# Hybrid decoder layer in fp32: product 5 of the convolution groups divided a second time

## What is computed

```python
h = rmsnorm(x, norm_g[layer])
proj = h @ w_in[layer]
b_a, c_a, x_a, z_a, q, k, v, z_b, g_a, g_b = jnp.split(proj, split_points, axis=-1)
# short_conv_branch
u = c_gate * xv
u = causal depthwise conv, 3 taps, + conv_b
y = b_gate * u * jax.nn.silu(z)
```

## Time and profile before

| | us |
|---|---|
| median of 3 runs | 1365.33 |
| lowest and highest | 1364.96, 1366.29 |
| profiled execution | 1364.82 |
| its span, first to last instruction | 1363.0 |
| TensorE busy | 1351.7 (99%) |
| VectorE busy | 1037.9 (76%) |
| ScalarE busy | 607.5 (45%) |
| GpSimd busy | 350.8 (26%) |

### The profile page before, as it was taken

One profiled execution on the slowest core, in us unless ns is written; L12 is line 12 of the kernel. 1 busy time (PEld: TensorE's weight loads), 2 busy tenths in 40 slices (PEclk: granted clock), 3 DMA queues, 4 the chain that ended last, 5 costly groups with the idle time before them and its releaser, 6 DMA issues.

```text
span 1363.0 us, 17225 instructions
## 1 busy us (share of the span) xinstructions
PE 1351.7 (99%) x6642; PEld 1143.1 (84%) x6642; DVE 1037.9 (76%) x1089; ACT 607.5 (45%) x823; POOL 350.8 (26%) x341
## 2 busy tenths in 40 slices
PE   9999999999999999999999999999999999999997
PEld 8788888888888888888888888888888888888886
DVE  7898466677777777677877777748776998788887
ACT  7843233433333333333433333438778443434445
POOL 0100122343444444223222233325544001100002
PEclk9999999999999999999999999999999999999999
DMA  9736545334443343466656556767767699935443
GB/s 343 214 126 213 152 107 169 89 103 109 109 109 84 102 108 94 131 177 177 178 157 174 149 156 183 216 209 252 269 217 263 151 331 306 237 152 201 165 83 124
DMA packets 112978, 234.80 MB, mean 172 GB/s; under 512 B 7680, under 2 KB 50816, under 8 KB 108032
## 3 DMA queue, kind: packets, MB, share of 16 engines
q1 hardware_dynamic: 104112, 194.87, 42.0%
q0 software_dynamic: 8640, 38.80, 16.0%
q10 hardware_dynamic: 144, 0.02, 0.0%
HBM read 169.70 MB, written 55.57 MB: 165 GB/s over the span
## 4 chain that ended last, share of the span: by engine, by line
PE 92%; ACT 2%; DVE 2%; issue 2%; DMA 1%; POOL 1%; SPq 1%; POOLq 0%; ACTq 0%; DVEq 0%
PE psum L2591 15%; PE psum L2593 15%; PE psum L2594 15%; PE psum L2732 7%; PE psum L2734 7%; PE psum L2733 7%; PE psum L2517 3%; PE psum L2519 3%; PE psum L2518 3%; PE psum L2506 3%; PE psum L2509 3%; PE psum L2508 3%; PE psum L2636 2%; PE psum L2638 2%; PE psum L2637 2%
## 5 line engine op out<-in xcount | busy, mean ns | idle before, releaser
L1126 ACT ACTIVATE slots<-work 128x1024 fp32r<-128x1024 f32 (+1 forms) x166 | 169.5, 1027 | 418.5 <-PE psum L2594 284.8
L2591 PE MATMUL psum<-hc,slots 128*128 128x512 f32 x912 | 354.9, 389 | 0.0
L2593 PE MATMUL psum<-hc,slots 128*128 128x512 f32 x912 | 354.9, 389 | 0.0
L2594 PE MATMUL psum<-hc,slots 128*128 128x512 f32 x912 | 354.8, 389 | 0.0
L2594 PEld LDWEIGHTS psum<-hc,slots 128*128 128x128 f32 x912 | 171.2, 188 | 35.7
L2591 PEld LDWEIGHTS psum<-hc,slots 128*128 128x128 f32 x912 | 171.3, 188 | 34.9
L2593 PEld LDWEIGHTS psum<-hc,slots 128*128 128x128 f32 x912 | 171.2, 188 | 34.8
L1412 ACT ACTIVATE last_slot<-arena 128x1024 fp32r<-128x1024 f32 x112 | 118.6, 1062 | 163.1 <-PE psum L2734 157.3
L2732 PE MATMUL psum<-last_slot 128*128 128x512 f32 (+1 forms) x452 | 175.3, 388 | 0.0
L2734 PE MATMUL psum<-last_slot 128*128 128x512 f32 (+1 forms) x452 | 175.0, 387 | 0.0
L2733 PE MATMUL psum<-last_slot 128*128 128x512 f32 (+1 forms) x452 | 175.0, 387 | 0.0
(11 more groups left out here) (225 smaller groups left out, 2424.1 us busy)
## 6 DMA issues: line engine op xcount, KB each, us to landing
work<-w_channel SPq DMA_DIRECT2D x80, 512.0 KB, 4.3
work<-w_channel POOLq DMA_DIRECT2D x40, 512.0 KB, 5.5
arena<-w_last SPq DMA_DIRECT2D x19, 1024.0 KB, 7.4
qk<-qk_scratch SPq DMA_DIRECT2D x32, 512.0 KB, 3.5
arena<-w_last POOLq DMA_DIRECT2D x9, 1024.0 KB, 11.0
v_raw<-value_scratch SPq DMA_DIRECT2D x32, 256.0 KB, 3.8
arena<-gate_scratch SPq DMA_DIRECT2D x16, 512.0 KB, 6.6
value_c<-w_value SPq DMA_DIRECT2D x10, 512.0 KB, 4.7
```

What stands on the lines that cost most here:

```text
L1126: nc.scalar.activation(slots[:, u % SLOTS, 0, 0:columns_of(u)], src, ACT.Copy, scale=-1.0 if negated(u) else 1.0).then_inc(w_hi, 1)
L2591: nc.tensor.matmul(bank, slot[:, 0, w], x_high, start=product in STARTS and j == 0, stop=False, skip_group_check=True)
L2593: nc.tensor.matmul(bank, slot[:, 0, w], x_low, start=False, stop=False, skip_group_check=True)
L2594: last = nc.tensor.matmul(bank, slot[:, 1, w], x_high, start=False, stop=j == 3, skip_group_check=True)
```

## The change

Product 5 is divided in the convolution groups (`FIFTHS = CONVS`). It gets a second unit, `FIFTH_HALF`, right behind its first; its T1, T2 and T4 lie in `hx`, where product 4's lie. So both sets are made in groups 0 and 1 and stored in DRAM (`hx_d`), and `hx` is loaded twice in every convolution group, for product 5 when product 4 of the group before has ended, for product 4 when product 5 has ended. T3 takes the place of a quarter of `hc`, saved and loaded back.

The sum S1 is no longer made by GpSimd from b and d, but by a transfer that adds quadrant 2 onto e, which is now loaded with quadrant 3 by itself; d is loaded separately, later. In convolution groups this transfer is issued ahead of GpSimd's sums for products 4 and 3, whose order is exchanged. GpSimd's sums for product 5 stand between its two products with the gate. VectorE's order changes: product 5's first slot right behind product 2's, the first tap waits for product 5's sums, product 5's second slot stands between the taps, the slots of products 7 and 3 follow the first subtraction of product 5, and product 4's first slot stands within its second subtractions. On ScalarE c11 moves behind product 3's first slot, and one SiLU of two columns is added at the start of group 2.

```diff
@@ -49,9 +49,10 @@
-LAST_HALF, THIRD_HALF = 7, 8
-UNIT_TABLE = [(g, p) for g in range(GROUPS) for p in (0, 1, 2, 3, 4, 5, 6, LAST_HALF, THIRD_HALF)
-              if (p != THIRD_HALF or g in THIRDS) and (p != LAST_HALF or g in TWICE)]
+FIFTHS = CONVS
+LAST_HALF, THIRD_HALF, FIFTH_HALF = 7, 8, 9
+UNIT_TABLE = [(g, p) for g in range(GROUPS) for p in (0, 1, 2, 3, FIFTH_HALF, 4, 5, 6, LAST_HALF, THIRD_HALF)
+              if (p != THIRD_HALF or g in THIRDS) and (p != LAST_HALF or g in TWICE) and (p != FIFTH_HALF or g in FIFTHS)]
...
 def halved_product(g, product):
 
-    return product == 4 and g in TWICE or product == 3 and g in THIRDS
+    return product == 4 and g in TWICE or product == 3 and g in THIRDS or product == 5 and g in FIFTHS
...
     g, n = place_of(u)
-    return 3 * QUARTER if n in (5, 6) and halved_product(g, product_at(n)) else 2 * HALF
+    return 3 * QUARTER if n in (3, 5, 6) and halved_product(g, product_at(n)) else 2 * HALF
...
@@ -189,10 +212,10 @@
 ROLES = [dict(a=0, b=1, c=2, d=3, e=4)]
 for _ in range(GROUPS - 1):
     r = ROLES[-1]
-    ROLES.append(dict(a=r["c"], b=r["b"], c=r["a"], d=r["e"], e=r["d"]))
+    ROLES.append(dict(a=r["c"], b=r["b"], c=r["a"], d=r["d"], e=r["e"]))
...
+    hx_d = nc.dram_tensor("hx_scratch", (2, P, 3, 2, 2, QUARTER), F32, kind="Internal").ap()
+    kept_d = nc.dram_tensor("kept_scratch", (4, P, 2, 2, QUARTER), F32, kind="Internal").ap()
...
     def second_bank(g, product):
 
-        return set_at(g + 1, 1 if g in THIRDS and product == 4 else 6)
+        return set_at(g + 1, 1 if product == 5 or g in THIRDS and product == 4 else 6)
...
+        def load_hx(product):
+            n = int(product == 5)
+            sp.dma_start(hx[:, 2].bitcast(F32), hx_d[n, :, 2]).then_inc(t4_in, 16)
+            sp.dma_start(hx[:, 0:2].bitcast(F32), hx_d[n, :, 0:2]).then_inc(t1_t2_in, 16)
+
         for g in range(GROUPS):
+            if g == 1:
+                sp.wait_ge(h_ready, made(3) + 4)
+                for part, a in enumerate((t5_high, t5_low)):
+                    sp.dma_start(hx_d[1, :, :, part], a[:, 0:3]).then_inc(fifth_kept, 16)
+                    sp.dma_start(kept_d[3, :, part], a[:, 3]).then_inc(fifth_kept, 16)
+                sp.wait_ge(fifth_kept, 112)
+                sp.wait_ge(h_ready, made(3) + 4 + 3)
+                sp.dma_start(hx_d[0], hx[:, :].bitcast(F32)).then_inc(fifth_kept, 16)
+            if g == FIFTHS.start:
+                sp.wait_ge(unit_done, unit_at(g - 1, 5) + 1)
+                sp.wait_ge(fifth_kept, 128)
+                for part in range(2):
+                    sp.dma_start(x_quarter(5, 1, part).bitcast(F32), kept_d[3, :, part]).then_inc(fifth_kept, 16)
+            if g in FIFTHS:
+                sp.wait_ge(unit_done, ended_at(g - 1) + 1)
+                load_hx(5)
+            if g == FIFTHS.stop:
+                sp.wait_ge(unit_done, fifth_ended_at(g - 1) + 1)
+                for part in range(2):
+                    sp.dma_start(x_quarter(5, 1, part).bitcast(F32), kept_d[2, :, part]).then_inc(fifth_kept, 16)
             if g == THIRDS.start:
                 stores[kind_of(g - 1)](g - 1)
             if g + 1 < GROUPS:
                 sp.wait_ge(w_ready, unit_at(g, 2) + 1)
-                sp.wait_ge(summed, summed_until(g) + 2)
+                sp.wait_ge(summed, s2_made(g))
                 load_work(g + 1, "a", 0)
...
             if g + 1 < GROUPS:
-                sp.wait_ge(w_ready, unit_at(g, 5) + 1)
-                load_work(g + 1, "d", 3)
+                sp.wait_ge(w_ready, fifth_ended_at(g) + 1)
+                load_work(g + 1, "e", 3)
                 sp.wait_ge(w_ready, unit_at(g, 7) + 1)
                 load_work(g + 1, "b", 2)
                 if g in THIRDS and g > THIRDS.start:
                     stores[kind_of(g - 1)](g - 1)
+                if g in FIFTHS:
+                    sp.wait_ge(unit_done, fifth_ended_at(g) + 1)
+                    load_hx(4)
+                if g in THIRDS:
+                    sp.wait_ge(w_ready, ended_at(g) + 1)
+                    load_work(g + 1, "d", 3)
                 sp.wait_ge(w_ready, third_ended_at(g) + 1)
                 load_work(g + 1, "c", 1)
             if g and g not in THIRDS:
                 stores[kind_of(g - 1)](g - 1)
+            if g + 1 < GROUPS and g not in THIRDS:
+                sp.wait_ge(w_ready, ended_at(g) + 1)
+                load_work(g + 1, "d", 3)
...
         def s1(g):
-            a, b, c, d, e = buffers(g)
+
+            if g:
+                work_loaded(g, "e")
+                pool.dma_start(work[ROLES[g]["e"]][:, :], w_channel[g, 2], accum_op=ALU.add).then_inc(s1_in, 16)
+            else:
+                a, b, c, d, e = buffers(g)
+                work_loaded(g, "b")
+                work_loaded(g, "d")
+                pool.wait_ge(w_ready, unit_of(1, 3, 1) + 1)
+                nc.gpsimd.tensor_tensor(e, b, d, ALU.add).then_inc(summed, 1)
+
+        def s3(g):
+
             work_loaded(g, "b")
-            work_loaded(g, "d")
-            pool.wait_ge(w_ready, ended_at(g - 1) + 1 if g else unit_of(1, 3, 1) + 1)
-            nc.gpsimd.tensor_tensor(e, b, d, ALU.add).then_inc(summed, 1)
-
-        def s3(g):
-
-            pool.wait_ge(summed, summed_until(g) + 1)
+            if g == 0:
+                pool.wait_ge(summed, summed_until(g) + 1)
             pool.dma_start(work[ROLES[g]["b"]][:, :], w_channel[g, 0], accum_op=ALU.add).then_inc(s3_in, 16)
 
         def s2(g):
             a, b, c, d, e = buffers(g)
+            if g:
+                pool.wait_ge(s1_in, 16 * g)
             pool.wait_ge(w_ready, unit_at(g, 1) + 1)
             nc.gpsimd.tensor_tensor(a, e, a, ALU.add).then_inc(summed, 1)
...
@@ -993,13 +1065,20 @@
             conv = g > 0 and kind_of(g - 1) == "conv"
             if conv:
                 conv_gate(g - 1, 1)
+            if g in FIFTHS:
+                second_sums(g, 5)
+            if conv:
                 conv_gate(g - 1, 2)
+            if g in FIFTHS:
+                s1(g + 1)
             if g in THIRDS:
+                second_sums(g, 4)
                 second_sums(g, 3)
-            if g in TWICE:
+            elif g in TWICE:
                 second_sums(g, 4)
             if g + 1 < GROUPS:
-                s1(g + 1)
+                if g not in FIFTHS:
+                    s1(g + 1)
                 s3(g + 1)
                 s2(g + 1)
...
-                    if product in (5, 6):
-                        act.wait_ge(summed, summed_until(g) + (5, 6).index(product) + 1)
+                    if product == 6:
+                        act.wait_ge(summed, s2_made(g))
+                    elif product == 5:
+                        act.wait_ge(s1_in if g else summed, 16 * g if g else summed_until(g) + 1)
...
+        def fifth_high():
+
+            act.wait_ge(t_made, 12 + 8)
+            for n in range(4):
+                nc.scalar.activation(t5_high[:, n].bitcast(F32R), t5_low[:, n], ACT.Copy).then_inc(h_hi, 1)
...
@@ -1558,8 +1648,11 @@
                 first(g)
             if p == 1 and g - 1 in CONVS:
                 first_tap(g - 1)
-            if p == 3:
+            if p == (FIFTH_HALF if g in FIFTHS and kind == "conv" else 3):
                 c11(g)
+            if g == CONVS.start and p == 1:
+                act.wait_ge(conv_step, 1)
+                nc.scalar.activation(u_pad[:, 0:CONV - 1], u_pad[:, 0:CONV - 1], ACT.Silu)
...
-        def second_rest(g, product):
-
-            dve.wait_ge(unit_done, (ended_at(g) if product == 4 else third_ended_at(g)) + 1)
+        def second_rest(g, product, parts=range(3)):
+
+            dve.wait_ge(unit_done, halved_ended_at(g, product) + 1)
             z = second_bank(g, product)
             to = flat((tp_v if product == 4 else tp_first)[g % 2][:, :, :]).rearrange("p (n c) -> p n c", n=4)
-            for n, (quarters, bank, c) in enumerate(((slice(1, 4), z, 0), (slice(1, 4, 2), z + 1, 0),
-                                                     (slice(2, 4), z + 1, QUARTER))):
+            for n in parts:
+                quarters, bank, c = ((slice(1, 4), z, 0), (slice(1, 4, 2), z + 1, 0), (slice(2, 4), z + 1, QUARTER))[n]
                 if n:
                     dve.wait_ge(value_sum, second_added(g, product, 1 + n))
...
@@ -2060,6 +2167,18 @@
                 g, n = place_of(u - 1)
                 if n in (5, 6) and halved_product(g, product_at(n)):
                     second_first(g, product_at(n))
+                    if n == 6 and g in FIFTHS and g not in THIRDS:
+                        low(u + 1)
+                elif n == 3 and halved_product(g, 5):
+                    second_first(g, 5)
+                elif n == FIFTH_HALF:
+                    second_rest(g, 5, range(1))
+                    if g in THIRDS:
+                        low(u + 2)
+                    second_rest(g, 5, range(1, 3))
+                    add(g, 5)
+                    if g not in THIRDS:
+                        low(u + 2)
```

(74 more changed lines are left out.)

63 lines of the change are left out of this document (41 added, 22 removed).

## The result

| | before | after |
|---|---|---|
| median, us | 1365.33 | 1368.54 |
| lowest and highest of 13 runs, us | 1364.89, 1367.01 | 1367.30, 1369.38 |
| profiled execution, us | 1364.82 | 1368.66 |
| its span, us | 1363.0 | 1366.8 |

What follows compares the result with a forecast made beforehand. TensorE, busy 1351.7 of 1363.0 us, was taken to bound the kernel. 1364.82 - 4.0 (matmuls) + 0.3 (one-off costs, late hx loads) = 1361.1 us profiled, 1361.6 as median; range 1360.6 to 1368.0.

Steps and rivals of the forecast that it cites:

- Removed matmuls: Product 5 divided on TensorE: 0.50 us less in each of eight groups, 4.0 us in all, at least 3.4.
- The work added on VectorE, ScalarE and GpSimd: Rearranged slots, sums and copies in each convolution group: costs nothing if the margins hold; the group ends at 36.68 us.
- the thinnest: VectorE's sum for product 5, done 4.9 us after product 7's start (Y), wanted at Y+5.44: 0.5 us to spare.
- Rival B: Product 5's chain on VectorE or ScalarE runs late for product 3 or 7; 0.5 us per group gives 1365.6; chance 0.16.
- The load of hx for product 4: Second hx load per convolution group: lands at Y+9.5 (Y: product 7's start), 0.2 us ahead of use; bounds Y+7.5, Y+11.7.
- Rival A: hx comes late, so TensorE stands before product 4's second half, eight times; chance 0.20 mildly, 0.08 severely.
- severe part: hx for product 4 late by 0.8 us or more per group: kernel slower, 1377 at 226 GB/s; chance 0.08.
- the mild case: hx for product 4 mildly late, 0.4 us per group: 1364.8 us; chance 0.20.
- Rival C: A single wait at the start or in the first convolution group costs 1.5 to 3 us: 1363 to 1364; chance 0.04.

Runs made afterwards that it cites:

- the order mended: Changed kernel with SP's loads of hx for product 4 ahead of b's load and y's store: 1361.28 us; with S1 also between GpSimd's sums for 4 and 3: 1361.05 us.
- S1 in the middle: Changed kernel with S1's transfer issued between GpSimd's sums for product 4 and those for 3, SP's order unchanged: 1361.9 us, ratio 0.9975.
- y twice: Changed kernel with y stored a second time, into a scratch nobody reads, ahead of the loads of hx: 1385.91 us, ratio 1.0150.
- y behind: Changed kernel with only y's store moved behind the loads of hx for product 4 on SP, b's load staying ahead: 1362.8 us, ratio 0.9982.
- S1 late: Changed kernel with S1's transfer put back behind GpSimd's sums for products 4 and 3, right ahead of S3's: 1377.37 us, ratio 1.0079.
- hx first: Changed kernel with the loads of hx for product 4 ahead of b's load and y's store in SP's queue: 1361.28 us, ratio 0.9969.
- S1 small: Changed kernel with S1's transfer at the same place moving only 128 of its 1024 columns in the convolution groups: 1361.71 us, ratio 0.9974.
- the best version: Changed kernel with hx loaded ahead of b's load and y's store, and S1 between GpSimd's sums for 4 and 3: 1361.05 us, ratio 0.9968.

## Why the prediction was wrong, point by point

- **Removed matmuls: right.** 0.51 us in each group for 0.50, and 4.93 us for product 5 against 4.94. The spacing of 117 to 118 ns from the trace held.
- **The work added on VectorE, ScalarE and GpSimd: right.** No margin ran out, not even the thinnest: in the group shown the sum for 5 ended at Y+4.7, for 4.9 expected and Y+5.44 wanted. The run without reloads shows it best: 36.68 us for the group of 36.68 of the forecast, with TensorE without a wait. Rival B had 0.16 of the chances and took nothing.
- **The load of hx for product 4: the step that failed.** The prediction had Y+9.5, "just in time"; it was Y+10.4, in seven groups of eight. Two terms of it were off. S1's transfer was to be issued at 18.5, which is Y-2.8, and to have 2 us of the engines left at Y. It was issued at Y-1.9, since it waits for the load of e, and it took 3.4 us of the engines until Y+3.5. While it ran, SP's queue hardly moved: 0.17 MB, though the sum let b, y and hx follow from Y-0.2 at the full rate in whatever S1 left. Set against it, the full rate itself was better than taken, 2.45 MB in 6.6 us, 371 GB/s, instead of 353. Together 0.9 us later, and the margin was 0.2.
- **Rival A** was the case, and with the right price: from 0.8 us late in each group, it said, the kernel is slower. The seven loads came 0.6 to 1.6 us late, 0.9 in the mean. What was wrong was its chance, 0.08 for that severe part against 0.52 for a step that was called the least certain by far and had its middle 0.2 us from the limit. With bounds of Y+7.5 and Y+11.7 around a use at Y+9.73, nearly half of the span lay on the late side; the chances should have followed it.
- **The range** ended at 1368.0, which was as far as the mild case went, and left the severe one out whole. The median is 1368.54.
- **Rival C** took little. The start of group 0 lies between 161.60 and 162.62 in ten profiled executions of the changed kernel and its variants, 162.0 in the mean, against 161.35 and 161.47 in the two of before. Some 0.6 us seem to belong to the change, in the value stage, which it doesn't touch. In nine of the ten, TensorE's waits show 0.3 to 0.9 us for a slot of VectorE there, once or twice, near 12 to 14 us or near 47; neither of the two of before shows one. With two executions of before that isn't proof, and why the slots come late is open.
- **Put together**, with the order mended, the kernel has the time that was forecast: 1361.05 and 1361.28 for 1361.6.

By the Trainium skill (DMA: Bandwidth & Descriptors, "Queues, rings and completion order") the DMA engines take turns between queues, packet by packet. Where both queues moved, from 336 to 337, the trace agrees: 36 packets of S1 and 39 of SP's queue. In the 3.5 us before that it doesn't: there were 99 of S1 and 2 of the other, whose first transfer had been issued at 332.5. The DMA view for 332.5:336, then for 336:337:

```profile
q0 software_dynamic: 99, 0.41, 79.0%
q1 hardware_dynamic: 2, 0.01, 0.6%
...
q0 software_dynamic: 36, 0.12, 59.7%
q1 hardware_dynamic: 39, 0.16, 45.1%
```

It is this late start that the sum lacked.

## What to carry to other kernels

When a new load must arrive in a window, list everything that is issued ahead of it on every queue, also on the other engine's, and count the accumulating transfers of GpSimd's queue at twice their bytes. Then ask which of them is in no hurry: here b, y's store and S1 all had microseconds to spare, and any one of three moves turned 0.2% slower into 0.2 to 0.3% faster. And if the middle of an estimate lies next to the limit, give the late side the share that the bounds give it.

## What the runs showed of the hardware

- **The accumulating transfers cost twice.** By the page's queue rows of the changed kernel 48.76 MB on GpSimd's queue took 19.8% of the engines' time, and 235.25 MB on the others took 49.3%: 5.6 and 2.9 us of the 16 engines for each MB. Packets of equal size, 4096 bytes, took 378 and 191 ns in the mean. Every transfer on GpSimd's queue here accumulates and none elsewhere does, so whether the adding costs it or the queue isn't shown.

```profile
q1 hardware_dynamic: 114320, 235.25, 49.3%
q0 software_dynamic: 11376, 48.76, 19.8%
```

- **A queue starts late behind another.** b's first packets came 2.7 to 3.6 us after its issue where S1 had the engines, 1.0 to 1.4 us after it where S1 was small, and 1.0 us after it with S1 in the middle, where nothing of S1 was under way.
- **A wait of TensorE can cost more than itself.** With y twice, TensorE's clock fell to 1.2 GHz behind single stops of 2.36 and 2.20 us and behind pairs (one for T4, one for T1 and T2, 0.8 us of matmuls between) of 1.61 and 1.60, 0.95 and 1.67, 0.16 and 2.03 us. Each fall cost 1.3 to 2.4 us more. It stayed at 2.4 GHz behind 1.17 and 1.63 us there, 1.8 us with y behind, all stops of the changed kernel (1.4 us at most, and a pair of 0.63 and 1.59 in its second profile), and also behind a single stop of 2.64 us with S1 late, the longest of all. So the length of the stop alone doesn't tell whether the clock falls. TensorE in that run, and the stretch behind it:

```profile
475.35 0.47 PE L2740 MATMUL psum<-hc,slots 128*128 128x512 f32 x1 [2.64 <-DVE slots L1746]
```
```profile
475.35:478.00 2.65, 2.65 (x12) 2.18 (x13) 2.51 (x3) 0.00 (x0) 1.62 (x2) 1.00 0.63 102
```

With y twice the profile puts some second stops down to a slot of VectorE: TensorE waits there for slot and load, and the slot had long been ready.

- **One group is mostly the latest.** In seven of the nine profiles with these loads, T1 and T2 landed last in the fourth convolution group, 1 to 3 us behind the usual group (in the changed kernel's first profile it was the sixth, with hx first the fifth). The program issues there what it issues in the others. It isn't SP's queue alone: with S1 small, what was left of S1 landed 5.5 us after its issue there and 2.7 to 4.4 us after it in the other groups. The cause is open, and in the best version this group alone has its load just in time.
